# Last 32 tokens' expert rows gathered and worked off on VectorE, dense experts for 224 tokens, one-hot rows four at once

## The chip, the core and the metric

The kernel runs on one core of a Trainium2 chip. The metric is the device time of one execution in microseconds (us). TensorE (PE) multiplies; before each product it loads a stationary matrix (weight load, PEld). VectorE (DVE), ScalarE (ACT) and GpSimd (POOL) do the elementwise work, SyncE (SP) issues the transfers from HBM. Each engine works its own instruction list in order, and waits in it on semaphores that the others raise.

## What is computed

Two transformer blocks over 256 tokens of width 1024. The change is in the feed-forward part of the first, a product-key mixture: each token has 8 heads, each head picks 16 of 16384 experts, so 128 chosen experts per token, with softmax weights g.

```python
q = (hc @ w_query).reshape(chunk, PEER_HEADS, PEER_QDIM)
s1 = einsum('thd,nd->thn', q[..., :half], k1)     # 128 keys each
s2 = einsum('thd,nd->thn', q[..., half:], k2)
v1, i1 = top_k(s1, 16); v2, i2 = top_k(s2, 16)
sc, pos = top_k(v1[..., :, None] + v2[..., None, :], 16)
eidx = i1 * 128 + i2 at pos
g = softmax(sc)
a = einsum('thkd,td->thk', expert_u[eidx], hc)
act = gelu(a) * g
out = einsum('thk,thkd->td', act, expert_v[eidx])
```

## The kernel before

Everything stands transposed: features on the 128 partitions, tokens in the free dimension. Weights come in slots of 512 KB (128 partitions x 1024 fp32). SP loads a slot into one of 4 RAW buffers (`NRAW`), ACT writes its high part (`split` in `act_program`, line 991) and DVE or POOL the low part (line 1372 on DVE, 2049 on POOL) into one of 3 SPL buffers (`NSPL`), always three slots ahead of PE. A product is made of three one-pass matmuls, high by high, high by low and low by high (`mm3`, line 553), so a slot of eight 128x128 blocks takes 24 matmuls, each with a weight load of its own. All PE work below goes through `mm` (line 551).

The experts are computed densely. 128 U slots give a = U h for 128 experts each, all 256 tokens wide; ACT applies Gelu into the store GB (line 1193 or, in place, 1196). 128 V slots then sum V times (gelu(a) g) into four PSUM banks. The gates g reach GB through one-hot products: for four tokens at a time DVE makes two 128x128 one-hot tables per token (`marks`, lines 1749 and 1750; the second is scaled by the gate), and PE multiplies each pair (`"g"` step, plain fp32, two passes). So there are 64 such blocks of 4 tokens. ACT stores the gates where U isn't there yet (line 1214), DVE multiplies where it is (`gated`, line 1759, and line 1827). Two buffers `oh` hold the tables of a block.

The order of this part is written out in `peer_steps()`, and each engine's program walks the same list: 48 U slots (`ROUTED`), with "turn" (transposing the selected indices) before the 47th; then blocks and U slots mixed, 76 U slots (`BESIDE`) over the blocks; the last U slots; then 128 V slots, with "a" steps, which split GB into high and low (asp, lines 1378 and 1375 on DVE), up to four ahead. Up to "turn" DVE also runs the top-16 routing. POOL makes low parts only until the 28th U slot (`LISTED`), then nothing until after the experts.

## Time and profile before

| | us |
|---|---|
| median of 3 runs | 1415.91 (1413.64 to 1417.72) |
| the profiled execution | 1414.68 |
| its span | 1412.6 |
| PE busy | 1383.5 (98%) |
| PEld busy | 1357.0 (96%) |
| DVE busy | 1006.8 (71%) |
| ACT busy | 692.0 (49%) |
| POOL busy | 392.5 (28%) |

The span is the time between the first and the last instruction of the profiled execution; "busy" is the time in which an engine has at least one instruction in work. "Idle before" in a row is the time that the engine stood just before that instruction, with what ended the wait behind the arrow. The granted clock is in parts of full speed: 1.00 is 2.4 GHz, 0.5 is 1.2 GHz.

### The profile page before, as it was taken

The numbers are of one execution on the slowest core, as the hardware profiler recorded it, in microseconds if no ns is written. First come the engines' busy times: TensorE is split into PE (matmuls) and PEld (weight loads), VectorE is DVE, ScalarE is ACT, GpSimd is POOL, SyncE is SP. The second block draws the span as 40 slices with busy tenths as digits, with TensorE's granted clock in tenths as the row PEclk, the third lists the DMA queues.
The fourth block names the chain that finished last, engine by engine and source line by source line (L and its number), as shares of the span: only waits on it lengthen the run. The fifth ranks groups of instructions, "written<-read, shape, count | busy, mean of one in ns | idle before, by whom it ended". The sixth has DMA issues, their size and how long they took to land.

```text
span 1412.6 us, 28033 instructions
## 1 busy us (share of the span) xinstructions
PE 1383.5 (98%) x11486; PEld 1357.0 (96%) x11486; DVE 1006.8 (71%) x2242; ACT 692.0 (49%) x1188; POOL 392.5 (28%) x185
## 2 busy tenths in 40 slices
PE   6999999999999999999999999999999999999998
PEld 6989899999999999999999999999999899999988
DVE  3573525859998898999966666776667954788743
ACT  5563446544454444444443333333345766656653
POOL 3744467678600000000000000000000553674332
PEclk9998999999999999999999999999999999999999
DMA  8433345555565444444455766556655534555553
GB/s 284 141 103 105 105 133 180 169 165 182 180 204 168 150 149 150 150 149 150 150 174 187 239 184 190 190 185 192 186 188 180 163 122 137 177 165 179 174 171 104
DMA packets 65095, 234.99 MB, mean 166 GB/s; under 512 B 7228, under 2 KB 7612, under 8 KB 64968
## 3 DMA queue, kind: packets, MB, share of 16 engines
q1 hardware_dynamic: 64968, 233.20, 51.8%
q8 instruction: 91, 1.49, 0.4%
q14 instruction: 36, 0.29, 0.1%
HBM read 232.13 MB, written 1.05 MB: 165 GB/s over the span
## 4 chain that ended last, share of the span: by engine, by line
PE 85%; DVE 9%; ACT 4%; issue 1%; DMA 0%; POOL 0%; SPq 0%; DVEq 0%; ACTq 0%
PE PS L551 84%; ACT SPL L991 2%; DVE SPL L1372 2%; DVE ub L2026 2%; DVE ub L2022 1%; DVE ub L2019 1%; PE PS L673 1%; DMA RAW<-in_dense 0%; DVE HF L1389 0%; DVE RS L1384 0%; DVE HS L1394 0%; DVE sb L1953 0%; ACT HS L1016 0%; DVE PS L1415 0%; DVE cosr L1915 0%
## 5 line engine op out<-in xcount | busy, mean ns | idle before, releaser
L991 ACT ACTIVATE SPL<-RAW 128x1024 fp32r<-128x1024 f32 x432 | 456.4, 1058 | 565.3 <-PE PS L551 561.9
L2049 POOL TENSOR_TENSOR SPL<-RAW,SPL 128x1024 fp32r<-128x1024 f32 x149 | 361.0, 2426 | 1000.8 <-ACT SPL L991 1000.7
L551 PE MATMUL PS<-HS,SPL 128*128 128x256 f32 x4656 | 572.8, 282 | 12.8 <-DVE SPL L1372 11.9
L551 PEld LDWEIGHTS PS<-HS,SPL 128*128 128x128 f32 x4656 | 554.2, 188 | 17.2 <-issue 15.7
L1372 DVE TENSOR_TENSOR SPL<-RAW,SPL 128x1024 fp32r<-128x1024 f32 x283 | 352.0, 1245 | 224.2 <-ACT SPL L991 223.1
L551 PE MATMUL PS<-asp,SPL 128*128 128x256 f32 x3072 | 358.7, 279 | 0.0
L551 PEld LDWEIGHTS PS<-asp,SPL 128*128 128x128 f32 x3072 | 358.5, 188 | 0.1
L551 PE MATMUL PS<-HXb,SPL 128*128 128x256 f32 x720 | 89.6, 285 | 1.9 <-DVE SPL L1372 1.3
L551 PEld LDWEIGHTS PS<-HXb,SPL 128*128 128x128 f32 x720 | 87.1, 189 | 3.1 <-DVE SPL L1372 2.1
L1750 DVE TENSOR_SCALAR oh<-CC,T3f 128x128 f32<-128x128 f32 x256 | 87.6, 342 | 0.0
L1749 DVE TENSOR_SCALAR oh<-CC,T3f 128x128 f32<-128x128 f32 x256 | 72.0, 281 | 0.0
L551 PE MATMUL PS<-oh 128*128 128x128 f32 x512 | 67.3, 274 | 0.0
L551 PE MATMUL PS<-actT,SPL 128*128 128x256 f32 x528 | 64.2, 284 | 3.1 <-DVE actT L1375 3.0
L551 PEld LDWEIGHTS PS<-actT,SPL 128*128 128x128 f32 x528 | 63.3, 192 | 4.0 <-DVE actT L1375 3.2
L551 PEld LDWEIGHTS PS<-oh 128*128 128x128 f32 x512 | 62.1, 191 | 0.0
L1375 DVE TENSOR_TENSOR asp<-GB,asp 128x256 fp32r<-128x256 f32 x128 | 54.3, 424 | 4.5
L551 PE MATMUL PS<-HXa,SPL 128*128 128x256 f32 x384 | 46.3, 281 | 0.7 <-POOL SPL L2049 0.7
L551 PEld LDWEIGHTS PS<-HXa,SPL 128*128 128x128 f32 x384 | 45.4, 188 | 0.9 <-issue 0.9
L1193 ACT ACTIVATE GB<-PS 128x256 f32<-128x256 f32 (+38 forms) x123 | 37.0, 301 | 0.0
L1378 DVE CAST asp<-GB 128x256 fp32r<-128x256 f32 x128 | 36.6, 286 | 0.0
L551 PE MATMUL PS<-SPL,HS 128*128 128x256 f32 x240 | 32.4, 296 | 0.0
L1759 DVE TENSOR_TENSOR GB<-GB,PS 128x192 f32<-128x192 f32 (+31 forms) x64 | 32.3, 506 | 0.0
(253 smaller groups left out, 1175.6 us busy)
## 6 DMA issues: line engine op xcount, KB each, us to landing
RAW<-in_dense SPq DMA_DIRECT2D x176, 512.0 KB, 3.6
RAW<-in_eu SPq DMA_DIRECT2D x128, 512.0 KB, 3.5
RAW<-in_ev SPq DMA_DIRECT2D x128, 512.0 KB, 4.2
bias<-in_nab SPq DMA_DIRECT2D x2, 768.0 KB, 8.3
XT<-in_xT SPq DMA_DIRECT2D x4, 256.0 KB, 5.5
out_y<-HF SPq DMA_DIRECT2D x4, 256.0 KB, 2.4
c<-in_c SPq DMA_DIRECT2D x1, 960.0 KB, 6.9
c<-in_c SPq DMA_DIRECT2D x1, 512.0 KB, 5.4
```

The costliest lines, as they stand in the source:

```text
L551: return e.matmul(out, l, r, start=start, stop=stop, skip_group_check=skip)
L673: t = e.transpose(ps[:, j, a * 128:a * 128 + 128], probs_of(tag, i)[:, a * 256 * chunks + c * 256 + j * 128: a * 256 * chunks + c * 256 + ...
L991: e.activation(spl(n)[0], raw(n), ACT.Copy).then_inc(*up("act_high", ("hi", n)))
L1193: e.activation(GB[:, i, t:T], ps[:, t:T], ACT.Gelu).then_inc(*up("act_gelu", ("gelu", i), *[("ev", "u", i)] * (t == 0)))
L1372: e.tensor_tensor(lo, raw(n), hi.bitcast(f32), ALU.subtract).then_inc(*up("dve_low", ("lo", n)))
L1375: return e.tensor_tensor(lo, x, hi.bitcast(f32), ALU.subtract).then_inc(*up("dve_part", *keys))
L1378: e.tensor_copy(hi, x).then_inc(*up("dve_part", ("phi", *keys[0])))
L1749: e.tensor_scalar(oh[m % 2][:, 0, j, :], con("iota"), T3f[:, 0, t:t + 1], None, ALU.is_equal)
L1750: q = e.tensor_scalar(oh[m % 2][:, 1, j, :], con("iota"), T3f[:, 1, t:t + 1], T3f[:, 2, t:t + 1], ALU.is_equal, ALU.mult)
L1759: e.tensor_tensor(GB[:, 0:n, 4 * m:4 * m + 4], GB[:, 0:n, 4 * m:4 * m + 4], psum("g", m).rearrange("p (t i) -> p i t", t=4)[:, 0:n, :], AL ...
L2026: e.tensor_tensor(uv[:, 0, :], uv[:, 0, :], uv[:, 1, :], ALU.mult).then_inc(*up("dve_conv", ("gated", f)))
L2049: e.tensor_tensor(lo, raw(n), hi.bitcast(f32), ALU.subtract).then_inc(*up("pool_low", ("lo", n)))
```

## The change

The last 32 tokens (TG) leave the dense part, which becomes 224 tokens (W) wide: the rows of `mm3` for U and V have 224 columns in place of 256, GB is 224 wide, and the one-hot blocks are 56 in place of 64. The 76 U slots beside them are spread over the 56.

For each of the 32 tokens the 128 chosen rows of U and of V (4 KB each, so twice 512 KB) are fetched by indirect DMAs from POOL. All POOL's 64 gathers stand at "turn", each waiting until the buffer is free (`dot` or `yrow` of the token before). In the V stage DVE takes token j at slot 107 j/31 rounded down: a product with sum of the U rows with the token's h (`dot`), then two slots later a multiply-add of the V rows into `yrow`. ACT does Gelu and the gate on a 128x1 column in between. The four groups of 32 partitions are four shares of chosen experts; 8 small fp32 products with `fold` (16 passes, 32 columns) add them to the PSUM banks ahead of the last V slot. Ahead of it `xrow`, h by token, is made from `copies` with 8 fp32 products (16 passes) at the 9th and 10th U slot.

The one-hot tables of a block are now one DVE instruction of 128x1024; the gate is put on the second table by ACT, four scaled copies of 128x128 (`weighed`). The high part of asp goes from DVE to ACT; the low part stays on DVE.

```diff
-    for m in range(T // 4):
+    for m in range(W // 4):
         yield "g", m
-        while (u - ROUTED) * (T // 4) < (m + 1) * BESIDE:
+        while (u - ROUTED) * (W // 4) < (m + 1) * BESIDE:
...
+def gather_slots():
+    return {j * 107 // (TG - 1): j for j in range(TG)}
...  (PE)
-                        t = mm3(ps[:, 0:256], (hi[:, c, :], lo[:, c, :]), rhs_h(c), c == 0, c == 7)
+                        t = mm3(ps[:, 0:W], (hi[:, c, :], lo[:, c, :]), (HS[:, 0, c, 0:W], HS[:, 1, c, 0:W]), c == 0, c == 7)
...
+                    if i in (8, 9):
+                        ps = take("scr", "xrow", i - 8)
+                        for c in range(4):
+                            w.wait_ge(*at("copies"))
+                            t = mm(ps[:, c * 128:c * 128 + 128], copies[:, 4 * (i - 8) + c, :], ident)
...
-                    w.wait_ge(*at("marks", i))
+                    w.wait_ge(*at("weighed", i))
...
+                        w.wait_ge(*at("yrow", TG - 1))
+                        for c in range(8):
+                            o = bank((0, 1, 4, 7)[c // 2])[:, (c % 2) * 256 + W:(c % 2) * 256 + 256]
+                            mm(o, yrow[:, c * 128:c * 128 + 128], con("fold"), False, False, True)
...
-                            t = mm3(bank((0, 1, 4, 7)[c // 2])[:, (c % 2) * 256:(c % 2) * 256 + 256],
-                                    (hi[:, c, :], lo[:, c, :]), (s[:, 0:256], s[:, 256:512]),
+                            t = mm3(bank((0, 1, 4, 7)[c // 2])[:, (c % 2) * 256:(c % 2) * 256 + W],
+                                    (hi[:, c, :], lo[:, c, :]), (s[:, 0:W], s[:, 256:256 + W]),
...  (ACT)
+            def weighed(m):
+                w.wait_ge(*at("marks", m))
+                w.wait_ge(*at("ev", "t3", 1))
+                for j in range(4):
+                    q = e.activation(oh[m % 2][:, 1, j, :], oh[m % 2][:, 1, j, :], ACT.Copy,
+                                     scale=T3f[:, 2, 4 * m + j:4 * m + j + 1])
+                q.then_inc(*up("act_weigh", ("weighed", m)))
...  (ACT, step "u")
+                    if i == ROUTED - 1:
+                        weighed(0)
+                        weighed(1)
+                elif what == "a":
+                    w.wait_ge(*at("gated4", W // 4 - 1))
+                    w.wait_ge(*at("ev", "u", i))
+                    if i >= 4:
+                        w.wait_ge(*at("v", i - 4))
+                    e.activation(asp[i % 4][:, 0:W], GB[:, i, :], ACT.Copy).then_inc(*up("act_part", ("ahi", i)))
...  (ACT, step "v")
+                    if i - 1 in beside:
+                        j = beside[i - 1]
+                        w.wait_ge(*at("dot", j))
+                        e.activation(hrow[:, j:j + 1], hrow[:, j:j + 1], ACT.Gelu).then_inc(*up("act_row", ("hgelu", j)))
+                        w.wait_ge(*at("hgelu", j))
+                        e.activation(hrow[:, j:j + 1], hrow[:, j:j + 1], ACT.Copy,
+                                     scale=grow[:, j:j + 1]).then_inc(*up("act_row", ("hrow", j)))
...  (ACT, step "g")
+                    if i < W // 4 - 2:
+                        weighed(i + 2)
...  (DVE)
-                for j in range(4):
-                    t = 4 * m + j
-                    e.tensor_scalar(oh[m % 2][:, 0, j, :], con("iota"), T3f[:, 0, t:t + 1], None, ALU.is_equal)
-                    q = e.tensor_scalar(oh[m % 2][:, 1, j, :], con("iota"), T3f[:, 1, t:t + 1], T3f[:, 2, t:t + 1],
-                                        ALU.is_equal, ALU.mult)
-                q.then_inc(*up("dve_mark", ("marks", m)))
+                e.tensor_tensor(oh[m % 2], con("iota").unsqueeze(1).unsqueeze(1).to_broadcast([128, 2, 4, 128]),
+                                T3f[:, 0:2, 4 * m:4 * m + 4].unsqueeze(3).to_broadcast([128, 2, 4, 128]),
+                                ALU.is_equal).then_inc(*up("dve_mark", ("marks", m)))
...  (DVE, step "v")
+                    if i in beside:
+                        j = beside[i]
+                        w.wait_ge(*at("urow", j))
+                        w.wait_ge(*at("ev", "xrow", 1))
+                        e.scalar_tensor_tensor(urow, urow, 1.0, xrow, ALU.mult, ALU.mult,
+                                               accum_out=hrow[:, j:j + 1]).then_inc(*up("dve_row", ("dot", j)))
+                    if i - 2 in beside:
+                        j = beside[i - 2]
+                        w.wait_ge(*at("vrow", j))
+                        w.wait_ge(*at("hrow", j))
+                        if j == 0:
+                            t = e.tensor_scalar(yrow, vrow, hrow[:, 0:1], None, ALU.mult)
+                        else:
+                            w.wait_ge(*at("yrow", j - 1))
+                            t = e.scalar_tensor_tensor(yrow, vrow, hrow[:, j:j + 1], yrow, ALU.mult, ALU.add)
...  (DVE, step "a")
-                    parts(asp[i % 4][:, 0:256], asp[i % 4][:, 256:512], GB[:, i, :], ("apart", i))
+                    w.wait_ge(*at("ahi", i))
+                    low_of(asp[i % 4][:, 0:W], asp[i % 4][:, 256:256 + W], GB[:, i, :], ("apart", i))
...  (POOL, step "turn")
+                    w.wait_ge(*at("erow"))
+                    for j in range(TG):
+                        at_ = bass.IndirectOffsetOnAxis(ap=erow[:, j:j + 1], axis=0)
+                        if j:
+                            w.wait_ge(*at("dot", j - 1))
+                        e.indirect_dma_start(urow, None, A["er"], at_).then_inc(*up("urow", ("urow", j), by=16))
+                        if j:
+                            w.wait_ge(*at("yrow", j - 1))
+                        e.indirect_dma_start(vrow, None, A["ev"].rearrange("a b c -> (a b) c"), at_).then_inc(
```

At "turn" DVE also writes the row numbers and gates of the 32 tokens (`chosen`, 8 instructions of 32x32), after the routing and ahead of its T3f copies. The loads of the constants of the second block move from the 22nd to the 25th V slot (`LATE`).

## Rows read from the trace of the kernel before

**Rows 1.** The page: busy time, granted clock by slices, chain that ended last.
```profile
PE 1383.5 (98%) x11486; PEld 1357.0 (96%) x11486; DVE 1006.8 (71%) x2242; ACT 692.0 (49%) x1188; POOL 392.5 (28%) x185
...
PEclk9998999999999999999999999999999999999999
...
PE 85%; DVE 9%; ACT 4%; issue 1%; DMA 0%; POOL 0%; SPq 0%; DVEq 0%; ACTq 0%
```

**Rows 2.** Busy time by stretch; us, instructions, clock, DMA share, GB/s.
```profile
310.00:440.00 130.00, 130.00 (x1107) 130.00 (x1106) 126.14 (x407) 64.91 (x96) 60.25 (x25) 1.00 0.59 185
440.00:716.00 276.00, 276.00 (x2390) 276.00 (x2390) 251.20 (x729) 123.34 (x297) 0.00 (x0) 1.00 0.47 149
722.00:1080.00 358.00, 358.00 (x3070) 357.95 (x3070) 242.41 (x403) 139.77 (x137) 0.00 (x0) 1.00 0.61 193
```

**Rows 3.** Instructions by tile: oh, then asp; duration min/median/max, first and last start.
```profile
L551 PE MATMUL PS<-oh x512: 270/275/275, 441.6 to 708.6; 128*128 128x128 f32 x171
...
L551 PEld LDWEIGHTS PS<-asp,SPL x3072: 186/188/189, 722.6 to 1081.0; 128*128 128x128 f32 x192
L551 PE MATMUL PS<-asp,SPL x3072: 274/280/357, 722.7 to 1081.1; 128*128 128x256 f32 x192
```

**Rows 4.** Timeline of weight loads: start, length of the merged group, count.
```profile
21.44 0.41 PEld L551 LDWEIGHTS PS<-CL,sqr 128*128 128x128 f32 x3
...
21.66 0.19 PEld L551 LDWEIGHTS PS<-CL,sqr 128*128 128x128 f32 x1
21.78 0.66 PEld L551 LDWEIGHTS PS<-HS,SPL 128*128 128x128 f32 x5
...
150.38 1.86 PEld L551 LDWEIGHTS PS<-probT,vd 128*64 128x64 f32 x9
...
501.57 0.97 PEld L551 LDWEIGHTS PS<-oh 128*128 128x128 f32 x8
502.46 0.66 PEld L551 LDWEIGHTS PS<-HS,SPL 128*128 128x128 f32 x5
```

**Rows 5.** The products of those weight loads: 2 and 256 moving columns.
```profile
L551 PE MATMUL PS<-CL,sqr 128*128 128x2 f32 x80 | 10.2, 233 | 0.0
L551 PE MATMUL PS<-probT,vd 128*64 128x256 f32 x48 | 11.2, 383 | 0.0
```

**Rows 6.** Timeline of DVE in the gate stage, one block with one U slot.
```profile
559.44 1.22 DVE L1372 TENSOR_TENSOR SPL<-RAW,SPL 128x1024 fp32r<-128x1024 f32 x1 [1.39 <-ACT SPL L991]
560.58 0.26 DVE L1827 TENSOR_TENSOR GB<-GB,PS 128x108 f32<-128x108 f32 x1
560.76 0.28 DVE L1749 TENSOR_SCALAR oh<-CC,T3f 128x128 f32<-128x128 f32 x1
560.96 0.34 DVE L1750 TENSOR_SCALAR oh<-CC,T3f 128x128 f32<-128x128 f32 x1
...
562.57 0.48 DVE L1759 TENSOR_TENSOR GB<-GB,PS 128x316 f32<-128x316 f32 x1
563.13 1.23 DVE L1372 TENSOR_TENSOR SPL<-RAW,SPL 128x1024 fp32r<-128x1024 f32 x1
```

**Rows 7.** Timeline of ACT in the same stage.
```profile
562.04 1.06 ACT L991 ACTIVATE SPL<-RAW 128x1024 fp32r<-128x1024 f32 x1 [2.06 <-PE PS L551]
563.01 0.27 ACT L1193 ACTIVATE GB<-PS 128x144 f32<-128x144 f32 x1
563.18 0.26 ACT L1196 ACTIVATE PS<-PS 128x112 f32<-128x112 f32 x1
563.36 0.32 ACT L1214 ACTIVATE GB<-PS 128x184 f32<-128x184 f32 x1
565.74 1.06 ACT L991 ACTIVATE SPL<-RAW 128x1024 fp32r<-128x1024 f32 x1 [2.06 <-PE PS L551]
```

**Rows 8.** Instructions of the forms that the change adds, or nearest to them.
```profile
L1667 DVE TENSOR_TENSOR eqs<-abf,CC x4: 2286/2287/2290, 383.5 to 412.4; 128x2048 f32<-128x2048 f32 x4
...
L1290 ACT ACTIVATE sb<-sb,sst 128x128 f32<-128x128 f32 x8 | 3.2, 395 | 6.4 <-DVE sst L1939 6.4
...
L1005 ACT ACTIVATE HS<-XT,CL x16: 492/494/512, 6.1 to 1084.6; 128x256 fp32r<-128x256 f32 x16
...
1083.44 1.70 ACT L1005 ACTIVATE HS<-XT,CL 128x256 fp32r<-128x256 f32 x4
...
L1788 DVE SCALAR_TENSOR_TENSOR sinr<-kq,ang 128x256 f32<-128x256 f32 x1 | 0.4, 419 | 0.0
```

**Rows 9.** Timeline of all engines in the V stage, one slot.
```profile
849.01 1.06 ACT L991 ACTIVATE SPL<-RAW 128x1024 fp32r<-128x1024 f32 x1 [1.74 <-PE PS L551]
...
850.10 1.23 DVE L1372 TENSOR_TENSOR SPL<-RAW,SPL 128x1024 fp32r<-128x1024 f32 x1 [0.91 <-ACT SPL L991]
851.24 0.29 DVE L1378 CAST asp<-GB 128x256 fp32r<-128x256 f32 x1
...
851.57 0.42 DVE L1375 TENSOR_TENSOR asp<-GB,asp 128x256 fp32r<-128x256 f32 x1
```

**Rows 10.** Timeline around "turn".
```profile
433.45 0.49 DVE L1740 TENSOR_TENSOR sel<-sel,ssum 128x128 f32<-128x128 f32 x2
...
435.31 0.82 PE L820 MATMUL PS<-CC,sel 128*128 128x128 f32 x6
...
436.66 1.22 DVE L1372 TENSOR_TENSOR SPL<-RAW,SPL 128x1024 fp32r<-128x1024 f32 x1 [1.58 <-ACT SPL L991]
```

**Rows 11.** DMA in the opening 30 us, in 40 slices, and two of its issues.
```profile
DMA  0088999979999999999999998300879999897300
GB/s 0 0 186 262 347 268 284 262 240 360 393 344 410 401 426 406 418 324 412 391 418 404 412 401 350 147 33 0 98 273 407 396 393 412 341 344 322 158 22 0
...
RAW<-in_dense SPq DMA_DIRECT2D x11, 512.0 KB, 5.8
bias<-in_nab SPq DMA_DIRECT2D x2, 768.0 KB, 8.3
```

**Rows 12.** DMA issues of the whole run: KB each, us from issue to landing.
```profile
RAW<-in_eu SPq DMA_DIRECT2D x128, 512.0 KB, 3.5
RAW<-in_ev SPq DMA_DIRECT2D x128, 512.0 KB, 4.2
```

More of the change, by code:

```diff
@@ L11 @@
 NE = 128
+TG = 32
+W = T - TG
+GROUPS = 128 // TG
 NRAW = 4
@@ L33 @@
 _at = 0
-for _n, _w in (("ident", 128), ("iota", 128), ("permd", 128), ("permr", 128)):
+for _n, _w in (("ident", 128), ("iota", 128), ("permd", 128), ("permr", 128), ("fold", TG)):
     C0[_n] = (_at, _w)
@@ L333, in build @@
         T3f = ex.take("T3f", 768).rearrange("p (b t) -> p b t", b=3)
+        rows = ex.take("rows", 2048)
+        xrow, yrow = rows[:, 0:1024], rows[:, 1024:2048]
+        copies = yrow.rearrange("p (c m) -> p c m", c=8)
+        urow = ex.take("urow", 1024)
+        vrow = ex.take("vrow", 1024)
+        hrow, grow, erow = RS[:, 0:TG], RS[:, TG:2 * TG], RS[:, 2 * TG:3 * TG].bitcast(u32)
         ar = Arena()
-        GB = ar.take("GB", NE * 256).rearrange("p (i t) -> p i t", t=256)
+        GB = ar.take("GB", NE * W).rearrange("p (i t) -> p i t", t=W)
         ar.close()
         ar = Arena()
-        ar.take("first", 58 * 256)
+        ar.take("before", ROUTED * W)
         keysT = ar.take("keysT", 256).rearrange("p (a n) -> p a n", a=2)
@@ L1199, in act_program @@
                         e.activation(sel[:, 2], sel[:, 2], ACT.Exp).then_inc(*up("act_exp", ("expg",)))
+                    if i == 6:
+                        w.wait_ge(*at("hn", 1, 7))
+                        e.activation(copies.rearrange("p c (g t) -> p c g t", g=GROUPS),
+                                     HF[:, :, W:T].unsqueeze(2).to_broadcast([128, 8, GROUPS, TG]),
+                                     ACT.Copy).then_inc(*up("act_copy", ("copies",)))
+                    if i in (9, 10):
+                        w.wait_ge(*at("full", "xrow", i - 9))
+                        e.activation(xrow[:, 512 * (i - 9):512 * (i - 9) + 512], psum("xrow", i - 9),
+                                     ACT.Copy).then_inc(*up("act_copy", ("ev", "xrow", i - 9)))
+                    if i == ROUTED - 1:
[7 more added lines that the diff above has]
+                    e.activation(asp[i % 4][:, 0:W], GB[:, i, :], ACT.Copy).then_inc(*up("act_part", ("ahi", i)))
                 elif what == "v":
@@ L1802, in angles @@
                     yield
-            routing, turning = route(), angles()
+            routing, turning, beside = route(), angles(), gather_slots()
             for _ in range(4):
@@ L1809, in dve_program @@
                     run(routing)
+                    w.wait_ge(*at("selected"))
+                    chosen()
                     for a in range(2):
@@ L1815, in dve_program @@
                     w.wait_ge(*at("ev", "t3", 1))
+                    w.wait_ge(*at("full", "xrow", 1))
                     marks(0)
@@ L2156, in _constants @@
     put(c0, C0, "ident", np.eye(128))
+    put(c0, C0, "fold", p[:, None] % TG == np.arange(TG)[None, :])
     put(c0, C0, "iota", np.arange(128)[None, :])
```

35 lines of the change are left out of this document (23 added, 12 removed).

## The prediction

> **What bounds the kernel now.** I read the page first [rows 1]: PE is busy 98% of the span, its clock is granted in full (2.4 GHz), and 85% of the chain that ended last is PE. Then the stretches [rows 2]: from 310 to 1080 us, the U slots, the gate blocks and the V slots, PE has no idle time at all. DVE is at 97% up to "turn", 91% in the gate stage and 68% in the V stage; ACT is at 39 to 50%, and POOL is idle from "turn" on. So PE sets the time of these 770 us and the others only have to keep up. What counts is first what one product costs PE, and second whether the others still keep up.
>
> The cost of a product: 3072 matmuls of the V stage start between 722.7 and 1081.1 [rows 3], 358.4/3071 = 116.7 ns apart. The gate stage runs from 441.6 to 722.7 = 281.1 us [rows 3] for 64 blocks and 80 U slots.
>
> **What 32 columns fewer give PE.** There is no one-pass matmul narrower than 256 columns in the trace. The nearest rows are plain fp32 ones. Weight loads in front of products with only 2 moving columns start at 21.44, 21.66 (two later) and 21.78, that is 110 to 120 ns apart; in front of 128 columns 8 of them take 502.46 - 501.57 = 0.89 us, 111 ns each [rows 4, 5]. A load of only 64 stationary columns can go faster, yet before 256 fp32 columns the spacing is 1.86 us for 9 [rows 4], over 200 ns: there the stream binds. So two limits stand side by side: the stream of moving columns, and a 128-column weight load, which takes 111 to 112 ns however short its product is. Today's 116.7 lies just above the second. Bounds for 224 columns: 111 and 116.7; I take 112, since three unlike products all end there. A gain of 4.7 ns, not the 14.6 that 32 of 256 columns suggest. The Trainium skill ("TensorE: Matmul & The Clock Gate", LDWEIGHTS) puts a load at its stationary columns over 1.2, here 107 ns; at that spacing stages 1 and 3 below would gain 21 us more and the sum be 1403, but the rows at 111 to 112 are this chip's.
>
> **Stage 1, the first 48 U slots.** 48 x 24 x 4.7 ns = -5.4 us. The 16 passes for xrow: +1.8 (111 ns each). The routing on DVE ends at 433.9 (433.45 + 0.49), only 1.4 us before PE transposes it at 435.3 [rows 10]; PE will come there 3.4 us earlier and DVE has 2 to 4 us of idle time to give in this stretch [rows 2], so I put +1.5. `chosen`, about 1.2 us of small instructions, is covered by the 1.58 us that DVE then waits for ACT [rows 10]. New is that block 0 needs `weighed(0)`, which stands on ACT behind the Gelu of U slot 47, which itself waits for the product just ahead of block 0 on PE: 0.36 + 4 scaled copies (1.2) + hand-overs, +2 once. Stage 1: -5.4 + 1.8 + 1.5 + 2 = 0.
>
> **Stage 2, the gate blocks.** PE's own work becomes 56 x 8 x 0.111 + 80 x 24 x 0.112 = 49.7 + 215.0 = 265 us. On DVE, one 128x1024 instruction replaces eight. By the 1024-column rows it gives its result after 1.22 us and frees DVE after 1.14 (559.44 to 560.58) [rows 6]; the 2048-column comparison with the same kind of broadcast takes 2.29 [rows 8], on the same line. Eight took (0.20 + 0.25) x 4 = 1.8 [rows 6]. So DVE's load falls. That is not what decides. Before, ACT waited in this stage only for PE. Now it waits for `marks(m+2)`, with its next `split` queued behind; and DVE's next `marks` is queued behind the low part of that split. This closes a ring across two engines that PE doesn't take part in:
>
> `marks` on DVE 1.25 (1.22 and the hand-over) -> four scaled copies on ACT -> high part to low part start 1.09 (849.01 to 850.10) [rows 9] -> low part 1.14 -> multiplication of the U slot 0.2 [rows 6] -> next `marks`.
>
> A scaled copy: 128x128 with a per-partition operand takes 395 ns, of 256 columns 494, and four of these in a row 1.70, so (1.70 - 0.49)/3 = 0.40 apart, 0.09 less than one alone [rows 8]. That puts 128 columns at 0.29 apart, 1.16 for four. Bounds: 0.18 apart, as the unscaled 128x112 that starts 0.18 before its follower [rows 7], and 0.32. I take 0.29, the row with the same operands.
>
> The ring takes 1.25 + 1.16 + 1.09 + 1.14 + 0.2 = 4.85 us for a block followed by one U slot (36 of 56), and 1.35 more, 6.2, for one followed by two (20). PE would need 0.89 + 2.69 = 3.58 and 6.27. So the ring is 1.27 us too slow in the single blocks, and the two oh buffers and three SPL buffers only lend a lead once. The mean of the slower in each is (36 x 4.85 + 20 x 6.27)/56 = 5.36. PE's block 54 comes 52 to 54 rings after block 0, then two blocks and 6 U slots, 17.9: 52 x 5.36 + 17.9 = 297 to 54 x 5.36 + 17.9 = 307. Going through the 56 blocks in the order of the programs with these durations gives 302. Stage 2: 302 - 281.1 = +21; without the ring it would be 265 - 281 = -16. Bounds from the copies alone: with 0.18 apart 280 (-1), with 0.32 309 (+28).
>
> **Stage 3, the V slots.** 128 x 24 x 4.7 ns = -14.4; 16 fold passes +1.8 (by the 2-column row): -12.6, if all others keep up with 2.69 us per slot. DVE today works 1.14 + 0.33 + 0.42 = 1.9 per slot [rows 9]. The cast goes to ACT, which stands 1.74 us per slot [rows 9]. `dot` and `yrow` have no row at 1024 columns; three-operand instructions of 256 columns take 419 ns like plain ones (424), so I take 1.14 to 1.3 each; 64 of them over 108 slots are 0.7 per slot. Together 1.14 + 0.38 + 0.7 = 2.2 of 2.69. No slot has both; a slot with one has about 2.7. The low part may come up to 5.4 us after the release of its buffer, and needs 2.2, so this is hidden.
> The gathers: 107 slots of 2.69 us carry 56 MB of slots and 33.5 MB of rows, 312 GB/s against 193 now [rows 2]; the opening held 400 to 426 GB/s over whole slices [rows 11]. A gather may start when its buffer is free and is needed 3 or 4 slots later, so at least 8.1 us. No row shows one from POOL. Slots of equal size land in 3.5 to 4.2 us [rows 12], in the crowded opening in 5.8, one of 768 KB in 8.3 [rows 11]. I take 6: hidden. The two 128x1 instructions of ACT fit into its 1.7 us.
> The Trainium skill ("DMA: Bandwidth & Descriptors", Anatomy of one DMA - SWDGE) gives 2.0 us + bytes/436e3 for a DMA from GpSimd, an estimate of 3.2 us here; no run yet shows it.
>
> **Sum.** 0 + 21 - 12.6 = +8.3 us on the profiled execution's 1414.7: 1423. The median lies 1.2 above it: 1424. What this says: PE is given some 36 us (6144 x 4.7 ns = 29, and 8 blocks = 7), and the ring takes it back in stage 2.
>
> **The rivals.** (a) The ring doesn't bind: the copies or the comparison are quicker than their rows, or ACT gets the tables early. For it: DVE's load falls by 0.7 us per block. Against: the order in both lists is fixed, each link has a row. Then stage 2 is 265, time 1424 - 37 = 1387; with copies at 0.18 apart 1402. (b) The weight load of one-pass matmuls is itself 116.7, and narrower products give nothing. For it: all forms with 256 columns stand at 116 to 117. Then stages 1 and 3 give back 20: 1444, slower. (c) The pace follows the columns, 116.7 x 224/256 = 102: stages 1 and 3 gain 176 x 24 x 9.9 ns = 42 more: 1382. The 2-column rows speak against it. The skill's page on TensorE (Back-to-back issue gap) has N/2.4 + 2.5 for a lone product, which would be 96 ns, but says itself that load and product together set the spacing. (d) The slow side: the gather. It decides from 8.1 us, between two takings of the buffer; past it DVE stands at `dot`, the low parts behind it in the list come late, and PE waits. Each us more costs about 31 us, once per token: 1455 at 9 us, 1486 at 10. For it: scattered rows, descriptors made by POOL, three streams at once. Against: 8.1 is twice what a slot takes. (e) A one-pass matmul under 256 columns falls to the price of fp32: two passes of 216 x 224/256 = 189 ns, +261 ns x 6144 = +1.6 ms, near 3000 us. No row excludes it. (f) The change doesn't do what it says: the gathered rows are not beside the V slots but ahead of them or behind, 32 x 2.5 us of DVE or more in the open, 1504 and up.
>
> **How the numbers follow.** This kernel's measurement can tell some 0.3% (4.2 us) from no change: "same" is 1411.7 to 1420.2. The forecast, ring at about its price, 0.44, with its own range 1407 to 1436: of it 0.04 faster, 0.12 same, 0.28 slower. (a) 0.22, in all its steps from 1387 to 1411: faster. (b) 0.10, slower. (c) 0.05, faster. (d) 0.12, slower. (e) 0.04, slower. (f) 0.03, slower. Faster 0.31, same 0.12, slower 0.57. The range reaches from (a) to (b) and the start of (d): 1386 to 1456, with (c), (e), (f) and the longer gathers outside.
>
> **What the profile of the changed kernel would show.** Matmuls into PS from asp,SPL 112 ns apart, with the same count. In the gate stage ACT waiting for DVE before the scaled copies (some 2 us per block), DVE waiting for ACT before line 1372's work, and PE idle by about 37 us there, released by ACT or DVE; first gate product to first V product 302. The one-hot instruction at 1.22, a scaled copy near 0.39. In the V stage PE without idle time, gathers landing within 8 us, DVE near 80%. If PE is busy in the gate stage throughout, the ring was wrong; if asp's spacing is 102 or 117, the weight load was; if DVE waits for DMA at `dot`, the gather was.

## The result, and the profile after

The change makes the kernel slower: median 1431.7 us (1426.6 to 1434.8, 4 runs) beside 1415.4 for the kernel before on the same chip, a ratio of 1.011 (95% interval 1.007 to 1.015). I had forecast 1424, range 1386 to 1456, and slower as the likeliest outcome.

The profiled execution of the kernel after took 1426.56 us, the shortest of its four; before it was 1414.68. The differences below are between these two executions. Lines of the kernel after: 569 is the matmul (551 before), 1019 the high part, 1437 the low part on DVE, 1812 the one-hot instruction, 1219 the scaled copy, 1902 the gate multiplication, 1912 `dot`, 1922 the multiply-add into `yrow`, 2172 and 2175 the gathers.

From the page of the kernel after: the span, the busy times, the clock by slices, the chain that ended last by engine and by line, and the landing of the V slots (us from issue to landing).

```profile
span 1424.5 us, 27951 instructions
PE 1362.9 (96%) x11454; PEld 1328.9 (93%) x11454; DVE 979.7 (69%) x1754; ACT 800.4 (56%) x1599; POOL 497.6 (35%) x249
PEclk9999999999999999999999999999999999999999
PE 49%; DVE 25%; ACT 11%; DMA 7%; issue 7%; SPq 0%; POOL 0%; DVEq 0%; ACTq 0%
PE PS L569 48%; ACT SPL L1019 6%; DVE SPL L1437 5%; DMA vrow<-in_ev,RS 4%; DVE oh L1812 4%; ACT oh L1219 4%; DVE ub L2114 2%; DMA urow<-in_er,RS 2%; DVE ub L2110 1%; DVE ub L2107 1%; DVE rows L1922 1%; DVE GB L1902 1%; DMA RAW<-in_ev 1%; DVE urow L1912 1%; PE PS L691 1%
RAW<-in_ev SPq DMA_DIRECT2D x128, 512.0 KB, 5.6
```

Against [rows 1] PE has lost 20.6 us of work and the span has grown by 11.9. PE's share of the chain falls from 85% to 49%. In its place come the members of the ring (lines 1019, 1437, 1812, 1219), and the two gathers with 6%. The row of tenths shows the clock granted in full nearly throughout, before and after; it hides a few short stretches at half clock, which matter below.

The stretches of the kernel after, in the columns of [rows 2]: the end of the first U slots, the gate stage, the V stage, and all that follows.

```profile
310.00:436.00 126.00, 125.58 (x1122) 125.21 (x1122) 124.36 (x404) 64.64 (x98) 61.72 (x27) 1.00 0.62 193
439.00:741.00 302.00, 273.46 (x2361) 266.99 (x2362) 195.45 (x271) 183.59 (x513) 0.00 (x0) 1.00 0.45 140
741.70:1090.00 348.30, 346.53 (x3089) 345.40 (x3088) 273.74 (x375) 187.49 (x325) 101.00 (x62) 1.00 0.85 293
1090.00:1424.00 334.00, 318.53 (x2558) 309.87 (x2556) 221.00 (x365) 196.27 (x360) 155.79 (x79) 0.99 0.48 153
```

And the products with asp, with the duration min/median/max and the first and last start, as [rows 3]:

```profile
L569 PE MATMUL PS<-oh x448: 275/275/377, 439.1 to 726.9; 128*128 128x128 f32 x150
L569 PE MATMUL PS<-asp,SPL x3072: 268/274/373, 741.8 to 1090.1; 128*128 128x224 f32 x192
```

With the starts of [rows 3] these lines cut each execution into four stretches, the last of which ends with the span; "spacing" in the table is the mean distance of neighbouring products with asp, without the few that PE waited for.

| kernel | to first gate product | gate stage | V stage | rest | spacing, ns |
|---|---|---|---|---|---|
| before | 441.6 | 281.2 | 358.4 | 331.4 | 116.7 |
| after | 439.1 | 302.7 | 348.3 | 334.3 | 111.7 |
| difference | -2.5 | +21.5 | -10.1 | +2.9 | |

The sum is +11.8, the 11.9 of the spans but for rounding. So PE got its cheaper products in the V stage, and the gate stage took back twice that.

The stretches at half clock (0.50, so 1.2 GHz) differ between the two executions, as long as PE has work, in two places. Windows around them, with PEclk third from the end; first from 126 to 138 us, before and then after, and then a window of the kernel after behind the experts:

```profile
126.00:138.00 12.00, 12.00 (x48) 10.02 (x47) 5.54 (x9) 0.69 (x1) 1.42 (x1) 0.57 0.24 82
126.00:138.00 12.00, 12.00 (x61) 10.19 (x60) 5.68 (x9) 2.11 (x4) 2.52 (x2) 0.72 0.25 83
1137.70:1141.00 3.30, 3.30 (x14) 3.12 (x15) 1.96 (x6) 0.00 (x0) 0.73 (x1) 0.50 0.70 240
```

The first stretch lasts 10.3 us before and 6.8 after; the second, 3.4 us from 1137.6 on, is missing before. At half clock the split products stand 213 ns apart where they stand 112 to 117 otherwise, so such a stretch costs a busy PE about half its length. My estimate is then 1.7 us gained in the first column of the table and 1.7 lost in "rest", neither by anything that the change does to PE's work there.

The waits of the gate stage of the kernel after: who waits for whom, us in total, times, longest.

```profile
ACT oh L1219 <- DVE oh L1812: 111.9, 54, 2.4
DVE SPL L1437 <- ACT SPL L1019: 106.1, 58, 2.6
PEld PS L569 <- DVE SPL L1437: 20.2, 17, 1.3
PE PS L569 <- DVE GB L1902: 17.4, 17, 1.1
PE PS L569 <- ACT oh L1219: 13.4, 15, 2.7
```

ACT waits for DVE 54 times, 2.07 us on average, and DVE for ACT 58 times, 1.83 us. Both engines are busy for under 65% of the stage (195 and 184 of 302 us), and yet PE runs dry. That is what a ring looks like: no member is full, each stands while it waits for another. One turn of it, on both engines (start, length, idle time before in brackets):

```profile
563.11 1.22 DVE L1812 TENSOR_TENSOR oh<-CC,T3f 128x1024 f32<-128x1024 f32 x1
564.25 0.48 DVE L1831 TENSOR_TENSOR GB<-GB,PS 128x312 f32<-128x312 f32 x1
564.37 1.28 ACT L1219 ACTIVATE oh<-oh,T3f 128x128 f32<-128x128 f32 x4 [2.07 <-DVE oh L1812]
565.55 1.04 ACT L1019 ACTIVATE SPL<-RAW 128x1024 fp32r<-128x1024 f32 x1
566.62 1.23 DVE L1437 TENSOR_TENSOR SPL<-RAW,SPL 128x1024 fp32r<-128x1024 f32 x1 [1.90 <-ACT SPL L1019]
567.76 0.25 DVE L1902 TENSOR_TENSOR GB<-GB,PS 128x96 f32<-128x96 f32 x1
567.93 1.22 DVE L1812 TENSOR_TENSOR oh<-CC,T3f 128x1024 f32<-128x1024 f32 x1
```

From `marks` to the next `marks` it takes 567.93 - 563.11 = 4.82 us. By the starts: 1.26 to the copies, 1.18 to the high part, 1.07 to the low part, 1.14 to the multiplication, 0.17 to the next `marks`.

In the V stage of the kernel after DVE waits for gathers. The waits of that stage:

```profile
DVE urow L1912 <- DMA urow<-in_er,RS: 24.9, 16, 3.5
ACT SPL L1019 <- DMA RAW<-in_ev: 14.2, 9, 2.3
DVE rows L1922 <- DMA vrow<-in_ev,RS: 10.8, 13, 2.2
```

The gathers, with the median us from issue to landing:

```profile
urow<-in_er,RS POOLq DMA_INDIRECT x32, 7.4
vrow<-in_ev,RS POOLq DMA_INDIRECT x32, 7.2
```

A gather can only start when the `dot` of the token before has given the buffer free. One turn of that, on DVE and POOL:

```profile
842.20 1.22 DVE L1912 SCALAR_TENSOR_TENSOR urow<-urow,rows 128x1024 f32<-128x1024 f32 x1 [3.45 <-DMA urow<-in_er,RS]
843.70 1.98 POOL L2172 DMA_INDIRECT urow<-in_er,RS  x1 [4.14 <-DVE urow L1912]
849.93 1.22 DVE L1912 SCALAR_TENSOR_TENSOR urow<-urow,rows 128x1024 f32<-128x1024 f32 x1 [0.81 <-DMA urow<-in_er,RS]
```

All 31 later gathers of `urow` are issued 1.50 us after the `dot` before them has started. Three slots of 24 products are 8.0 us, which leaves 6.5 for the gather, and four slots are 10.7, which leaves 9.2. Of the 31 distances between tokens 17 have three slots and 14 have four. DVE's 16 waits for `urow` all stand at the ones with three; those with four have none.

Of the 35.7 us that DVE stands there for both tiles, little reaches PE: 3071 distances of 111.7 ns are 343.0 us, the 16 passes of the fold measure 1.9, and 348.3 - 343.0 - 1.9 = 3.4 us are left as gaps of PE.

### The profile page after: what moved, and what is told of

Its sections match the earlier page's. It is cut to its first block, busy times and chain, and to the rows that moved or that the text cites. A ratio compares the mean times of both kernels' runs of the same rounds, so it can differ in the third digit from the quotient of the medians.

```text
span 1424.5 us, 27951 instructions
## 1 busy us (share of the span) xinstructions
PE 1362.9 (96%) x11454; PEld 1328.9 (93%) x11454; DVE 979.7 (69%) x1754; ACT 800.4 (56%) x1599; POOL 497.6 (35%) x249
## 4 chain that ended last, share of the span: by engine, by line
PE 49%; DVE 25%; ACT 11%; DMA 7%; issue 7%; SPq 0%; POOL 0%; DVEq 0%; ACTq 0%
PE PS L569 48%; ACT SPL L1019 6%; DVE SPL L1437 5%; DMA vrow<-in_ev,RS 4%; DVE oh L1812 4%; ACT oh L1219 4%; DVE ub L2114 2%; DMA urow<-in_er,RS 2%; DVE ub L2110 1%; DVE ub L2107 1%; DVE rows L1922 1%; DVE GB L1902 1%; DMA RAW<-in_ev 1%; DVE urow L1912 1%; PE PS L691 1%
## 5 line engine op out<-in xcount | busy, mean ns | idle before, releaser
L569 PE MATMUL PS<-HS,SPL 128*128 128x224 f32 (+1 forms) x4656 | 555.0, 278 | 30.6 <-DVE GB L1902 17.4
L569 PE MATMUL PS<-asp,SPL 128*128 128x224 f32 x3072 | 345.1, 275 | 1.8 <-DVE SPL L1437 1.5
L2172 POOL DMA_INDIRECT urow<-in_er,RS x32 | 52.6, 1645 | 449.7 <-DVE urow L1912 392.8
L1219 ACT ACTIVATE oh<-oh,T3f 128x128 f32<-128x128 f32 x224 | 71.6, 391 | 111.9 <-DVE oh L1812 111.9
L2175 POOL DMA_INDIRECT vrow<-in_ev,RS x32 | 51.0, 1593 | 105.2 <-DVE rows L1922 100.9
L1812 DVE TENSOR_TENSOR oh<-CC,T3f 128x1024 f32<-128x1024 f32 x56 | 68.2, 1219 | 0.5 <-PE PS L569 0.5
L1912 DVE SCALAR_TENSOR_TENSOR urow<-urow,rows 128x1024 f32<-128x1024 f32 x32 | 39.1, 1222 | 24.9 <-DMA urow<-in_er,RS 24.9
L1440 DVE TENSOR_TENSOR asp<-GB,asp 128x224 fp32r<-128x224 f32 x128 | 49.5, 386 | 1.7 <-ACT asp L1255 1.7
L1255 ACT ACTIVATE asp<-GB 128x224 fp32r<-128x224 f32 x128 | 47.8, 373 | 0.1
L1922 DVE SCALAR_TENSOR_TENSOR rows<-vrow,RS,rows 128x1024 f32<-128x1024 f32 x31 | 39.7, 1281 | 10.8 <-DMA vrow<-in_ev,RS 10.8
```

Source lines behind the costliest of these rows:

```text
L569: return e.matmul(out, l, r, start=start, stop=stop, skip_group_check=skip)
L1219: q = e.activation(oh[m % 2][:, 1, j, :], oh[m % 2][:, 1, j, :], ACT.Copy, scale=T3f[:, 2, 4 * m + j:4 * m + j + 1])
L1255: e.activation(asp[i % 4][:, 0:W], GB[:, i, :], ACT.Copy).then_inc(*up("act_part", ("ahi", i)))
L1440: return e.tensor_tensor(lo, x, hi.bitcast(f32), ALU.subtract).then_inc(*up("dve_part", *keys))
L1812: e.tensor_tensor(oh[m % 2], con("iota").unsqueeze(1).unsqueeze(1).to_broadcast([128, 2, 4, 128]), T3f[:, 0:2, 4 * m:4 * m + 4].unsqueeze( ...
L1912: e.scalar_tensor_tensor(urow, urow, 1.0, xrow, ALU.mult, ALU.mult, accum_out=hrow[:, j:j + 1]).then_inc(*up("dve_row", ("dot", j)))
```

## The experiments

All times are medians; the ratio is that to the kernel before, which was timed beside each. Its medians were 1415.3 to 1415.7. The table holds the stages of the profiled executions, cut as above.

| kernel | to first gate product | gate stage | V stage | rest | time, us | ratio (95%) |
|---|---|---|---|---|---|---|
| late | 440.9 | 267.5 | 348.2 | 332.8 | 1390.3 | 0.982 (0.980 to 0.985) |
| oldmarks | 439.2 | 264.5 | 348.5 | 334.4 | 1387.7 | 0.980 (0.978 to 0.982) |
| onehot | 443.2 | 334.2 | 358.4 | 331.3 | 1470.6 | 1.039 (1.037 to 1.041) |
| onehot_late | 443.0 | 282.8 | 358.4 | 331.3 | 1418.5 | 1.003 (1.002 to 1.004) |
| widths | 436.1 | 273.7 | 343.1 | 331.3 | 1386.6 | one run |
| widths2 | 439.0 | 282.0 | 348.2 | 333.6 | 1405.4 | one run |
| nogather | 439.3 | 305.6 | 344.9 | 335.0 | 1426.3 | 1.008 (1.006 to 1.009) |
| old_spread | 438.8 | 264.5 | 344.9 | 334.5 | 1384.7 | 0.979 (0.977 to 0.980) |
| old_spread_pad32 | 438.1 | 264.5 | 344.9 | 333.0 | 1382.6 | one run |
| old_spread_pad96 | 436.7 | 264.5 | 344.9 | 332.9 | 1382.2 | 0.977 (0.976 to 0.978) |

The profiled executions differ in the clock too, and a stage has to be read with that. Five kernels (after, late, onehot, onehot_late, nogather) let PE stand 2.7 us for `weighed(0)` just ahead of the first gate product. In the kernel after the clock stays full behind it; in the others it is at half, for 6.8 us in late and nogather and for 3.4 in onehot and onehot_late. And 47 us behind the last product with asp no product starts for 2.9 to 3.0 us, in all twelve kernels; behind that the clock is at half for 3.4 us in seven (after, oldmarks, nogather, widths2 and the three old_spread) and full in five (before, late, onehot, onehot_late, widths). The head of the gate stage of late, then of nogather:

```profile
440.90:447.20 6.30, 6.30 (x29) 6.30 (x30) 1.90 (x2) 1.47 (x5) 0.00 (x0) 0.50 0.69 231
439.30:445.40 6.10, 6.06 (x28) 6.09 (x29) 1.92 (x2) 2.78 (x9) 0.00 (x0) 0.50 0.68 242
```

**Is it the ring, or the cost of the instructions in it?** `late` keeps every instruction of the kernel after and moves only ACT's four copies in its list: behind the high part and the Gelu of the next U slot, so that DVE's low part no longer waits for them.

```diff
+                    while owed:
+                        weighed(owed.pop())
...
-                    if i < W // 4 - 2:
-                        weighed(i + 2)
+                    owed = [i + 2] if i < W // 4 - 2 else []
```

> The changed kernel with one thing moved: ACT scales block m+2's table behind the next U slot's high part and Gelu, not ahead of them. Nothing else differs, all instructions stay. Ring theory: ACT's next high part no longer waits for DVE's comparison, so the ring is open and PE sets the gate stage again: first gate product to first V product 265 us in place of 302.6, spacing of the products still 112 ns, total 1432 - 38 = 1394 us. Rival, the stage is slow because ACT and DVE simply have more or slower work (copies, comparison): the same instructions stay, so the stage stays near 300 and the time near 1430.

Measured 1390.3 us. ACT's waits for `oh` are gone, and of PE's one is left, the first (waits of the gate stage of late):

```profile
ACT SPL L1019 <- PE PS L569: 78.9, 66, 4.4
DVE SPL L1438 <- ACT SPL L1019: 68.0, 79, 4.7
PE PS L569 <- ACT oh L1219: 2.7, 1, 2.7
```

The same 224 scaled copies and 56 comparisons now cost PE almost nothing: the gate stage falls from 302.7 to 267.5 us. That is 3.0 above `oldmarks` below, where PE never waits, and 6.8 us at half clock are enough for it (an estimate of 3.4). It was the order of ACT's list, not the size of any instruction.

`oldmarks` undoes the one-hot part alone: eight 128x128 instructions per block on DVE, no `weighed`.

> The changed kernel with the one-hot part undone: DVE makes the tables of a block with eight instructions, gate included, and ACT scales nothing; width 224, 56 blocks, gathers stay. Ring theory: no ring, but DVE is loaded by 0.66 us more per block and then just about as long as PE in the blocks with one U slot (3.6 us both): gate stage 265 to 270 us, total 1392 to 1400. If the one-hot part were the gain and the width or the gathers the loss, this kernel would be slower than the changed one, above 1435.

Measured 1387.7, some 4 us under the range that I had expected. The gate stage is 264.5 us with PE busy throughout (264.40 of 264.40 us):

```profile
439.30:703.70 264.40, 264.40 (x2369) 264.40 (x2370) 234.99 (x658) 122.21 (x295) 0.00 (x0) 1.00 0.51 163
```

DVE is busier there than in the kernel after (235 us against 195) and PE never waits. So DVE's load, which the new one-hot instruction relieves, was not in short supply.

**The ring on the kernel before.** `onehot` is the complement: the one-hot part alone, 256 columns, no gathers (lines as in the kernel before, 1191 is the copy). `onehot_late` is the same with `late`'s order.

> The kernel before with the one-hot part alone: one comparison on DVE and four scaled copies on ACT per block, 256 columns, 64 blocks, no gathers. Ring theory: 4.85 us per block with one U slot (52 of 64) against 3.69 of PE, so the gate stage grows from 281 to about 332 us and 2.7 us are lost once at its start: 1415 + 54 = 1469 us. Rival, the loss of the changed kernel comes from the width or from the gathers: then this one stays at 1415 or below.

> The kernel before with the one-hot part alone, and ACT's scaled copies put behind the next U slot's Gelu: the ring opened, at 256 columns and 64 blocks. Ring theory: the gate stage, 334 us with the ring, falls back to PE's own 281 us; what stays is the 2.7 us in front of block 0, where ACT scales only after the Gelu of the U slot just ahead. 1415.4 + 2.7 = 1418 us. Rival, the copies themselves load ACT or the SBUF ports so that PE or the splits are slowed: well above 1420.

Waits of the gate stage of onehot:

```profile
ACT oh L1191 <- DVE oh L1761: 127.6, 62, 2.5
DVE SPL L1386 <- ACT SPL L991: 121.7, 66, 4.1
PE PS L551 <- ACT oh L1191: 33.6, 37, 2.7
```

The part alone makes the kernel 55 us slower, with the ring's signature. Of 64 blocks 52 have one U slot behind them and 12 two; 52 x 4.85 + 12 x (0.89 + 2 x 2.80 = 6.49) is 330 us, or 5.16 per block. Counted as in the prediction, 60 to 62 such blocks and then two blocks of PE with the last 6 U slots (18.6 us), the stage comes to 328 to 338 us; it took 334.2. With the copies moved, 52 us of the 55 are gone; 3 are left, 1.4 of them ahead of the first gate product and 1.6 behind it, where 3.4 us at half clock account for about 1.7. So the one-hot part brings nothing even without the ring: it takes work off an engine that had time to spare.

**What does a narrower product cost?** `widths` is the kernel before with other widths: the expert products take 240 columns for U and 160 for V, nothing else is changed, and the last 16 and 96 tokens' share of those products is left out. `widths2` has 252 and 248 columns and leaves out that of the last 4 and 8.

```diff
-  t = mm3(ps[:, 0:256], (hi[:, c, :], lo[:, c, :]), rhs_h(c), c == 0, c == 7)
+  t = mm3(ps[:, 0:240], (hi[:, c, :], lo[:, c, :]), (HS[:, 0, c, 0:240], HS[:, 1, c, 0:240]), c == 0, c == 7)
...
-          (hi[:, c, :], lo[:, c, :]), (s[:, 0:256], s[:, 256:512]),
+          (hi[:, c, :], lo[:, c, :]), (s[:, 0:160], s[:, 256:416]),
```

> The kernel before with narrower expert products: 240 moving columns in the U slots, 160 in the V slots (the last 16 and 96 tokens are left out of them). Weight-load theory: a one-pass product can't come faster than its 128-column weight load, so both are 111 to 112 ns apart like those with 224, a gain of 6144 x 4.9 ns = 30 us, 1385 us. Rival, the stream of columns sets the pace: 109 to 112 ns at 240 and 73 to 80 ns at 160, about 1275 us. A third, a slow mode below some width, would show as a spacing over 117.

> The kernel before with 252 moving columns in the U slots and 248 in the V slots (the last 4 and 8 tokens are left out of them). Two limits side by side: the stream costs its columns at 2.4 per ns plus what 256 columns show beyond that (116.7 - 106.7 = 10 ns), and no product comes closer than 111.7. That gives 115.0 ns at 252 and 113.3 at 248, and the two limits cross near 244 columns, so that of 32 columns only the first 12 pay. If the spacing drops to 111.7 as soon as it is under 256, the 256 itself is special (place or length of the rows), not the stream.

The products with asp (duration min/median/max, first and last start), first of widths:

```profile
L551 PE MATMUL PS<-asp,SPL x3072: 240/275/314, 709.8 to 1052.8; 128*128 128x160 f32 x192
```

then of widths2:

```profile
L551 PE MATMUL PS<-asp,SPL x3072: 273/277/354, 721.0 to 1069.2; 128*128 128x248 f32 x192
```

343.0/3071 = 111.7 ns with 160 columns, the same as with 224: between these widths the columns don't count at all. The U slots of widths, with 240, show 112.8 without the waits, a little over the 111 to 112 that I had expected. With 248 it is 348.2/3071 = 113.4, as I expected (113.3). The 252 columns missed: I had expected 115.0, and in the first 48 U slots they are 116.7 ns apart. A stretch of 100 us of U slots alone, from 330 to 430, holds 859 products:

```profile
330.00:430.00 100.00, 100.00 (x859) 100.00 (x858) 98.25 (x246) 50.16 (x75) 42.21 (x18) 1.00 0.61 189
```

PE has no idle time in it, and only one distance there is over 130 ns, so it is PE's own pace: 252 columns cost what 256 cost. The same stretch of the kernel before holds 851. Its first 48 U slots have 117.8 ns between products, those of onehot 116.7, though onehot does the same work there with its tiles at the same places. So 256-column products can be 1 ns slower for a reason that these runs don't show.

**How much of it are the gathers?** `nogather` fetches only the first token's rows and lets all 32 tokens use them; DVE, ACT and PE do the same work. That leaves out the rows of the other 31 tokens.

```diff
-                        w.wait_ge(*at("urow", j))
+                        w.wait_ge(*at("urow", 0))
...
-                    for j in range(TG):
+                    for j in range(1):
```

> The changed kernel with POOL fetching rows for the first token only; DVE and ACT do the row work of all 32 tokens on whatever stands in the buffers (the result of the last 32 tokens is wrong by that). Theory: the V stage loses 3.5 us in the profiled run (PE gaps while DVE stands before a gather that takes 7.4 us of the 8.1 there are), and this is also what makes its runs differ by 8 us. So V stage 348.3 -> 345, gate stage unchanged at 302, time 1431.7 - 3.5 to 6 = 1426 to 1428, runs within 3 us of each other. Rival, the row work itself on DVE and ACT delays the low parts: V stage stays at 348.

The V stage of nogather:

```profile
744.90:1089.80 344.90, 344.90 (x3089) 344.80 (x3088) 274.89 (x375) 187.22 (x325) 0.00 (x0) 1.00 0.65 201
```

and its two gathers, with the us from issue to landing:

```profile
urow<-in_er,RS POOLq DMA_INDIRECT x1, 5.0
vrow<-in_ev,RS POOLq DMA_INDIRECT x1, 5.3
```

344.9 us = 343.0 + 1.9, PE without a gap: the 3.4 us of gaps in the kernel after come from the gathers, and DVE's row work (275 us of 345) hides in full. The two gathers are issued at 434.5 and 435.9 us, ahead of the gate stage and one over the other, beside the U slots (242 GB/s from 434.3 to 441 us). The first two of the kernel after, at the same place, land in 4.5 and 5.6 us. In its V stage, at 293 GB/s, the medians are 7.4 and 7.2, so crowding is the likely cause of the longer landing; no run varies it alone. The median fell by 5.4 us (1431.7 to 1426.3), but the two profiled executions are 0.5 us apart the other way: -3.4 in the V stage, +2.9 in the gate stage, +0.7 behind it. The gate stage has the same instructions in both; here it starts with 6.8 us at half clock, there it doesn't. The four runs lie 1.7 us apart, where those of the kernel after lie 8.3 apart. That doesn't pin the spread on the gathers: the four of late, with gathers, lie 6.2 apart, and the ten of onehot_late, without, 4.6.

**Can the gaps be had back?** `old_spread` takes oldmarks and gives each token more slots: token j at V slot 121 j/31 in place of 107 j/31, so 3.9 slots per token instead of 3.45. To make room the loading of ACT's tables for the next block moves from the V slots 8 and 16 ahead of the end to the last two. Both edits are in it.

```diff
-    return {j * 107 // (TG - 1): j for j in range(TG)}
+    return {j * 121 // (TG - 1): j for j in range(TG)}
...
-                    if i == NE - 8:
+                    if i == NE - 1:
...
-                    if i == NE - 16:
+                    if i == NE - 2:
```

> The kernel with the one-hot part undone (1387.7), and the 32 tokens at slot 121 j/31 in place of 107 j/31, so that most gathers have 4 slots (10.7 us) and three only 3 (8.1 us); the two table changes of ACT for the next block move from slots 112 and 120 to 126 and 127. Theory as for the run without gathers: V stage 348.5 -> 345, 1384 us. Rival, the gathers slow the slots' own loads by the load on the DMA engines (landing 5.6 in place of 4.2 us), and that is what costs: same bytes in nearly the same time, so V stage stays within 1 us of 348.5.

Waits of DVE in the V stage of old_spread:

```profile
DVE urow L1901 <- DMA urow<-in_er,RS: 3.4, 4, 2.3
DVE rows L1911 <- DMA vrow<-in_ev,RS: 2.9, 4, 1.2
```

DVE waits 6.3 us for rows in place of 27.5 in oldmarks (35.7 in the kernel after), and the V stage is 344.9, as without gathers. Of the 17 distances of three slots 3 are left. So 13% more distance between the tokens is enough. What the moved tables add was not told apart, but nogather has them at their old place and PE without a gap. The five runs lie 0.6 us apart, those of oldmarks 2.3.

**What is longer behind the experts?** The work there is not touched, and yet "rest" is 2.9 us longer after the change. The products with mixT (192 of 256 columns) show it: duration min/median/max, first and last start, of the kernel before:

```profile
L551 PE MATMUL PS<-mixT,SPL x192: 277/280/470, 1180.9 to 1204.2; 128*128 128x256 f32 x192
```

of the kernel after:

```profile
L569 PE MATMUL PS<-mixT,SPL x192: 277/283/468, 1191.7 to 1215.6; 128*128 128x256 f32 x192
```

Their mean spacing without the waits is 116.7 ns before and 119.9 after; those with actT go from 116.8 to 118.5, those with HXb from 119.2 to 119.8. Products with HS, whose tile stands ahead of the constants in SBUF, hardly move (116.9 and 117.3 behind the experts). The change adds the constant `fold`, 32 columns of 4 bytes, and all tiles behind it move by 128 bytes (mixT and HXb by 16 KB more, for the row buffers ahead of them). So I put unused columns behind the tile RS until the move is 512 bytes (96 more columns) and 256 bytes (32 more); the 16 KB stay.

```diff
         RS = top_.take("RS", 256)
+        top_.take("pad", 96)
```

> The same with 96 unused columns behind RS, which moves every later tile by 384 bytes more: with the 32 columns of fold, 512 in all. Theory from the trace: after the experts, 256-column products are 117.6 to 119.9 ns apart in the changed kernel where they were 116.6 to 118.5 (mixT 119.9 against 116.7, actT 118.5 against 116.8), and the 128 bytes by which fold moved the tiles are the cause. If the place counts and 512 bytes restore it, the stage behind the experts falls from 334.3 to 331.5 us and the time by 2.5 to 1381.5. If the place doesn't count, nothing changes.

> The same with 32 unused columns, so 256 bytes in all. One look at the spacing of the products behind the experts (mixT, actT, HXb): 116.7 for mixT if 256 bytes restore it too, 119.9 or another value if not.

The same products of old_spread_pad96:

```profile
L570 PE MATMUL PS<-mixT,SPL x192: 277/280/470, 1147.4 to 1170.6; 128*128 128x256 f32 x192
```

Spacing 116.7 again with either padding, actT 116.7, HXb 119.0 and 119.3. The spacing of mixT is shown cleanly: 119.9 in all five kernels with the 128 bytes, 116.7 in the five without and the two padded. The time falls by 2.5 us to 1382.2 (1380.3 to 1383.4, five runs). That the sum came out as expected is in part luck. I had expected "rest" to fall by 2.8, to 331.5; in the profiled executions it falls by 1.6. Another 2.1 us go ahead of the gate stage, of which about 1.7 are the clock (at half for 10.2 us from 126.7 on in old_spread, for 6.8 from 127.4 on in old_spread_pad96) and 0.3 the 384 products with HXa, 117.8 ns apart in the one and 117.1 in the other.

So the tiles' places are worth about 1.5 us of "rest", and the half clock behind the wait of PE about as much. Four kernels show it: before 331.4 us (nothing moved, clock full there), late 332.8 (moved, full), widths2 333.6 (nothing moved, half) and the kernel after 334.3 (both). Products of 224 columns have 111.7 ns wherever their tiles stand. This version is the fastest of all, 33.2 us below the kernel before, with the narrow experts and the gathers kept and the one-hot part dropped.

## Why the prediction was right, and where it was not

**The bound and the spacing.** Right. PE was the limit, and a 224-column product costs 111.7 ns where I took 112. Rival (b), nothing gained at 116.7, (c), pace by columns at 102, and (e), the price of fp32, are gone: 160 columns cost 111.7 too. The page on TensorE that I had weighed, the Trainium skill's "TensorE: Matmul & The Clock Gate" (LDWEIGHTS), gives 107 ns for the load; the runs show a spacing of 111.7, so the rows of the trace were the better guide. By my estimate from that page's figure the change would have gained another 4.7 ns x 6144 = 29 us.

**Stage 2.** Right in mechanism and size. Ring 4.85 forecast, 4.82 in the turn shown; scaled copies 0.29 apart forecast, (1.28 - 0.39)/3 = 0.30 measured; comparison 1.22; stage 302 forecast, 302.7 measured. (By its own rows the term for the copies should have been 0.395 - 0.09 = 0.305 apart and not 0.29; that lay inside its bounds.) Rival (a), that the ring doesn't bind, is refuted by `late` and `oldmarks`: opened, the stage takes 267.5 and 264.5. What I had given rival (a) as its time, 1387, is close to what both reach (1390.3 and 1387.7).

**Stage 1.** Forecast 0, measured -2.5. The +1.5 for the routing didn't arise. DVE ended it at 429.3 (428.83 + 0.49), and PE transposed at 430.3, without a wait:

```profile
428.83 0.49 DVE L1805 TENSOR_TENSOR sel<-sel,ssum 128x128 f32<-128x128 f32 x2
...
430.26 0.82 PE L844 MATMUL PS<-CC,sel 128*128 128x128 f32 x6
...
437.72 2.44 ACT L1219 ACTIVATE oh<-oh,T3f 128x128 f32<-128x128 f32 x8
...
439.13 1.13 PE L569 MATMUL PS<-oh 128*128 128x128 f32 x8 [2.70 <-ACT oh L1219]
```

I had treated DVE's routing as fixed in time with 2 to 4 us to give; it finished 4.6 us earlier than in [rows 10], so it went along with PE's faster slots. The wait for `weighed(0)` was 2.7 us where I took 2. Of the -2.5, 1.0 lies ahead of the first U slot (it starts at 305.2 us before, 304.2 after), where the shorter half clock gives about 1.7 and the products with HXa, 118.0 ns apart where they were 116.9, take back 0.5. The stretch from there to the first gate product went from 136.4 to 135.0 us: -6.1 ns x 1152 = -7.0 (117.8 to 111.7, the U slots of the kernel before being slower than its V slots), +1.8 for xrow, +0.7 in two waits for a low part, +2.7 for `weighed(0)`, which adds up to -1.8, where -1.4 was measured. So the forecast of 0 missed by a routing term that was not there, and by a clock that no step had in it.

**Stage 3.** Forecast -12.6, measured -10.1. The product's part was a little better than forecast, -15.4 at 111.7 ns. The step that failed is the overlap of the gathers, "at least 8.1 us" against "I take 6: hidden", and both its terms were off. The gathers land in 7.4 us at the median (4.5 to 9.3), above what I had read off slots of equal size; the slots beside them land later too (5.6 us against 4.2 in [rows 12]). And the 8.1 us counted from one `dot` to the next, but the buffer is held for the first 1.5 of them, so 6.5 are left. The median gather is thus 0.9 us too late at each distance of three slots, 17 of 31. So rival (d) is there at small size, 3.4 us in this execution. Its limit, 8.1 us of landing, was too high, and its price, 31 us for each us over, far too high: DVE stood 35.7 us in all, and PE lost a tenth of that, because the low parts have time to give. DVE's own load was right: near 80% forecast, 273.7 of 348.3 us measured, 79%. For the gather's landing I had cited the Trainium skill's "DMA: Bandwidth & Descriptors" (Anatomy of one DMA), which gives an estimate of 3.2 us; the fastest gather of this run took 4.5.

**Not seen.** +2.9 us behind the experts, half of it from where tiles stand in SBUF, half from 3.4 us at half clock. No step of the prediction looked at the addresses of tiles that the change moves, and it read the clock as granted in full from a row of tenths.

**The sum.** Forecast +8.3 on the profiled execution, measured +11.9: 0 against -2.5, +21 against +21.5, -12.6 against -10.1, and nothing against +2.9. That the total is near is partly luck: stage 1 and what lies behind the experts missed by nearly the same amount in opposite directions, and the clock's share in the two (-1.7 and +1.7) cancels. The median then lay 5.1 us above the profiled execution where I had put 1.2, since the kernel after spreads over 8 us. The spread of nogather is 1.7 us and that of old_spread 0.6, but with four or five runs each, and 6.2 in late, what the spread comes from stays open. The clock behind PE's wait for `weighed(0)` is one candidate: it was full in the profiled execution of the kernel after, its fastest, and at half in those of the four others with that wait.

## What to carry to other kernels

When an operation is split over two engines that each work a fixed list, write down the cycle of who waits for whom, over the items that stand between in both lists, and compare its length with the bound engine's pace: here 4.82 us against 3.58 cost 38 us, no engine in it was full, and moving four copies behind the next item in one list gave back 35 of them. Relieve only an engine that is short: the cheaper one-hot tables brought nothing, while the narrower products and the gathers brought 33 us. Give an asynchronous fetch some slack past its crowded time and not its quiet one (7.4 and about 5 us here), and count its time from when the buffer comes free, not from when it was last taken (6.5 us of 8.0). After an edit that adds a constant, look at the spacing of the untouched products behind it. And before a difference of 1 to 3 us between two executions is given a cause, compare the granted clock in short windows: the page's row of tenths, with 35 us to a digit, doesn't show it.

## What the runs showed of the hardware

- The spacing of one-pass fp32 products with a weight load of 128 columns each is 111.7 ns with 160 or 224 moving columns, 112.8 with 240, 113.4 with 248 and 116.7 with 252 and 256: a floor, and a steep end. At half clock it is 213 ns.
- With 256 columns the spacing also depends on the address of a tile: 116.7 ns for mixT, and 119.9 with all tiles moved by 128 bytes. A move by 256 or 512 bytes leaves it at 116.7. Which operand it is was not told apart; products with HS, which didn't move, stayed at 116.9 to 117.3. Why it is so is open. It is not the only thing: HS products of the U slots were 117.8 ns apart in one kernel and 116.7 in another with its tiles at the same places.
- Where no product had started for 2.9 to 3.0 us, the granted clock then stood at half (1.2 GHz) for 3.4 or 6.8 us in some executions and stayed full in others: ahead of the gates at half in four of five, behind the experts in seven of twelve. The runs don't show what decides.
- A gather of 128 rows of 4 KB by one indirect DMA lands 4.5 to 5.6 us after issue beside the slots alone (242 GB/s with the gathers), and in 7.4 at the median in the V stage at 293 GB/s in all. In the kernel after POOL is busy for 0.9 to 2.3 us with each.
